# Memory attention of both layers in eight units of two heads, its sample sequences in 32-row blocks

## The reference, cut to what matters

```python
def memory_attention(qm, g_q_mem, mem_k, mem_v):
    B, L, _ = qm.shape
    q = rms_norm(qm.reshape(B, L, H_MEM, HD_MEM), g_q_mem)
    s = jnp.einsum('blhd,bmhd->bhlm', q, mem_k).astype(jnp.float32) * (HD_MEM ** -0.5)
    p = jax.nn.softmax(s, axis=-1)
    return jnp.einsum('bhlm,bmhd->blhd', p, mem_v).reshape(B, L, D_MEM)
```

## Time and profile before

| | us |
|---|---|
| median of 3 runs (2698.41 to 5250.33) | 2704.03 |
| the profiled execution, its whole time | 2707.99 |
| its span, first to last instruction | 2706.3 |
| TensorE busy in the span | 2585.6 (96%) |
| VectorE busy | 1182.1 (44%) |
| ScalarE busy | 810.8 (30%) |
| mean granted clock of TensorE, share of full speed | 0.965 |

### The profile page before, as it was taken

One profiled execution on the slowest core, in us unless ns is written; L12 is line 12 of the kernel. 1 busy time (PEld: TensorE's weight loads), 2 busy tenths in 40 slices (PEclk: granted clock), 3 DMA queues, 4 the chain that ended last, 5 costly groups with the idle time before them and its releaser, 6 DMA issues.

```text
span 2706.3 us, 44423 instructions
## 1 busy us (share of the span) xinstructions
PE 2585.6 (96%) x18995; PEld 2459.4 (91%) x18995; DVE 1182.1 (44%) x1455; ACT 810.8 (30%) x1019; POOL 101.5 (4%) x205
## 2 busy tenths in 40 slices
PE   6999999999988799999999999999998879999998
PEld 6999999999755599999999999999986559999998
DVE  7333335583354334433454343334543734443343
ACT  5222223443122323222233322222334633222222
POOL 1000000000112100000000100000011020000000
PEclk9999999999889789999999999999997989999999
DMA  5222322222212122223222322322232042223222
GB/s 175 82 85 73 91 80 75 62 67 80 60 56 74 61 63 78 74 82 93 72 68 94 115 78 81 87 80 70 89 121 75 26 146 78 78 69 102 78 60 84
DMA packets 334523, 220.74 MB, mean 82 GB/s; under 512 B 11849, under 2 KB 326497, under 8 KB 334420
## 3 DMA queue, kind: packets, MB, share of 16 engines
q1 hardware_dynamic: 325268, 185.83, 23.8%
q0 software_dynamic: 9152, 33.43, 3.8%
HBM read 206.78 MB, written 12.45 MB: 81 GB/s over the span
## 4 chain that ended last, share of the span: by engine, by line
PE 92%; DVE 5%; ACT 1%; issue 1%; DMA 1%; SPq 0%; POOLq 0%; POOL 0%; DVEq 0%; ACTq 0%
PE psum L519 73%; PE psum L545 6%; PE psum L2156 1%; PE psum L1443 1%; PE psum L1502 1%; PE psum L1494 1%; PE psum L1757 1%; PE psum L1483 1%; PE psum L1740 1%; PE psum L2379 1%; PE psum L1474 0%; PE psum L2202 0%; PE psum L1708 0%; PE psum L2185 0%; DMA x_nat<-in_x_sample 0%
## 5 line engine op out<-in xcount | busy, mean ns | idle before, releaser
L519 PE MATMUL psum<-act_hi,whi 128*128 128x288 f32 (+2 forms) x3504 | 756.1, 298 | 12.4 <-DVE act_lo L786 3.8
L519 PE MATMUL psum<-act_hi,wlo 128*128 128x288 f32 (+2 forms) x3504 | 753.8, 297 | 0.0
L519 PE MATMUL psum<-act_lo,whi 128*128 128x288 f32 (+2 forms) x3504 | 753.1, 297 | 0.0
L519 PEld LDWEIGHTS psum<-act_hi,whi 128*128 128x128 f32 (+2 forms) x3504 | 563.7, 188 | 15.3 <-issue 4.9
L519 PEld LDWEIGHTS psum<-act_lo,whi 128*128 128x128 f32 (+2 forms) x3504 | 564.0, 188 | 0.3
L519 PEld LDWEIGHTS psum<-act_hi,wlo 128*128 128x128 f32 (+2 forms) x3504 | 563.4, 187 | 0.4
L498 DVE TENSOR_TENSOR wlo<-raw,whi 128x2048 fp32r<-128x2048 f32 x190 | 435.4, 2292 | 238.7 <-ACT whi L491 238.5
L491 ACT ACTIVATE whi<-raw 128x2048 fp32r<-128x2048 f32 x190 | 362.0, 1905 | 272.6 <-PE psum L519 268.6
L519 PE MATMUL psum<-h_lo,whi 128*128 128x288 f32 x1408 | 301.9, 295 | 0.0
L519 PE MATMUL psum<-h_hi,wlo 128*128 128x288 f32 x1408 | 301.9, 295 | 0.0
L519 PE MATMUL psum<-h_hi,whi 128*128 128x288 f32 x1408 | 301.9, 295 | 0.0
(11 more groups left out here) (410 smaller groups left out, 2143.2 us busy)
## 6 DMA issues: line engine op xcount, KB each, us to landing
raw<-in_w_ffn_up SPq DMA_DIRECT2D x176, 512.0 KB, 5.0
raw<-in_w_ffn_down SPq DMA_DIRECT2D x64, 384.0 KB, 3.9
raw<-in_w_ffn_down SPq DMA_DIRECT2D x64, 320.0 KB, 3.4
raw<-in_w_out SPq DMA_DIRECT2D x16, 512.0 KB, 4.4
raw<-in_w_in_a SPq DMA_DIRECT2D x14, 512.0 KB, 4.7
raw<-in_w_in_a SPq DMA_DIRECT2D x16, 384.0 KB, 4.0
raw<-in_w_kv SPq DMA_DIRECT2D x12, 512.0 KB, 4.1
vpg<-in_cache_v POOLq DMA_DIRECT2D x16, 384.0 KB, 4.0
```

Of the source, the lines that this page charges most:

```text
L519: last = pe.matmul(psum[0:width, 4 * j + 2 * m + h, 0:HALF], w[:, k, cols], a[:, k, h * HALF:(h + 1) * HALF], start=(k == 0 and step == 0) ...
```

## The change

Both layers' prompt part goes by eight units u: 128 tokens (u // 2) and the two heads of one half of the partitions (heads u % 2 and 2 + u % 2). There are four slots for scores (PSUM banks 0 to 3), for the exponentials `ma_e` (in `spare_hi`) and for the turned ones `ma_pt` (in `spare_lo`), two for transposes (banks 4, 5) and outputs (banks 6, 7). The sample part turns keys 0 to 3 between units 4 and 7, keeps all 8 sequences' keys in SBUF (copied in place, half by ACT and half by DVE), makes scores and outputs of four sequences in four 32-partition blocks, the values streamed 256 columns wide, and turns the 128 x 256 result back in two transposes. The norm of the last mLSTM head moves on DVE behind the sample softmax of A. A's query norm uses the functions of B. A's memory loads move from POOL to SP, behind the state loads; the constants' making on POOL moves into the last head of the mLSTM; B's loads are all issued at once.

```diff
@@ PE @@
+            def scores(u):
+                t, rows = u // 2, slice(64 * (u % 2), 64 * (u % 2) + 64)
+                if u >= 4:
+                    pe.wait_ge(S.ma_exp, 8 * l + u - 3)
+                for x in range(2):
+                    last = pe.matmul(mem_scores(u)[:, x, :], B.qn[rows, x, t * P:(t + 1) * P], mk_t[l][rows, x, :],
                                      start=True, stop=True)
+            def turn(u):
+                pe.wait_ge(S.ma_p, 8 * l + u + 1)
+                if u >= 2:
+                    pe.wait_ge(S.ma_pt, 8 * l + u - 1)
+                for y in range(4):
+                    last = pe.transpose(psum[:, 4 + u % 2, y * P:(y + 1) * P], ma_e[:, u % 4, y // 2, (y % 2) * P:(y % 2 + 1) * P],
+                                        ident[:, :])
+            def outputs(u):
+                pe.wait_ge(S.ma_pt, 8 * l + u + 1)
+                if u >= 2:
+                    pe.wait_ge(S.ma_out_lo, 10 * l + u - 1)
+                for x in range(2):
+                    for m in range(2):
+                        h = 2 * x + u % 2
+                        last = pe.matmul(mem_mix(u)[:, x, :], mv[l][:, m, h * DM:(h + 1) * DM], ma_pt[:, u % 4, 2 * x + m, :],
+                                         start=(m == 0), stop=(m == 1))
+            def sample_scores(g):
...
+                for pair in range(2):
+                    for x in range(4):
+                        last = pe.matmul(psum[32 * x:32 * x + 32, 4 + g, 0:M], B.qz[:, pair, 4 * g + x, :],
+                                         keys_turned(B, 4 * g + x)[:, pair, :], start=(pair == 0), stop=(pair == 1),
+                                         skip_group_check=True)
+            def sample_outputs(g):
+                pe.wait_ge(S.ms_pt, 2 * l + g + 1)
+                pe.wait_ge(S.ma_out_lo, 10 * l + 7 + g)
+                for m in range(2):
+                    for x in range(4):
+                        last = pe.matmul(psum[32 * x:32 * x + 32, 6 + g, 0:M], ma_pt[:, g, m, 32 * x:32 * x + 32],
+                                         B.vs[:, 4 * g + x, m, :], start=(m == 0), stop=(m == 1), skip_group_check=True)
+            for u in range(4):
+                scores(u)
...
+            turn(0)
+            for u in range(8):
+                if u + 1 < 8:
+                    turn(u + 1)
+                if u + 4 < 8:
+                    scores(u + 4)
+                if u == 4:
+                    turn_keys(0)
+                    turn_keys(1)
+                if u == 6:
+                    turn_keys(2)
+                    turn_keys(3)
+                outputs(u)
+            sample_scores(0)
+            for b in range(4, 8):
+                turn_keys(b)
+            sample_scores(1)
+            for g in range(2):
+                turn_sample(g)
+                sample_outputs(g)
+            for g in range(2):
+                turn_back(g)
@@ ACT @@
+            exponents(0)
+            exponents(1)
+            for u in range(8):
+                if u + 2 < 8:
+                    exponents(u + 2)
+                copy_turned(u)
+                if u == 6:
+                    copy_keys(0)
+                if u:
+                    mixed_hi(u - 1)
+            copy_keys(1)
+            mixed_hi(7)
+            copy_keys(4)
+            copy_keys(5)
...
@@ DVE @@
             maxima(0)
+            hooks[0]()
+            maxima(1)
+            hooks[1]()
+            maxima(2)
+            for u in range(8):
+                weights_of(u)
+                if u + 3 < 8:
+                    maxima(u + 3)
+                if u == 3:
+                    place_memory_queries()
+                if u:
+                    mixed_lo(u - 1)
+            copy_keys(2)
+            copy_keys(3)
+            mixed_lo(7)
+            copy_keys(6)
+            copy_keys(7)
             for g in range(2):
+                sample_maxima(g)
+                sample_weights(g)
+            hooks[2]()
+            for g in range(2):
+                copy_outputs(g)
+            for g in range(2):
+                sample_lo(g)
@@ DVE, layer A @@
-            qnorm_dve(dve, 0, 2, 0, lambda k: qm_a[:, k, :], lambda k: MA.qn[:, k, :], lambda k: vec_t[:, 72:73])
-            head_norm_dve(dve, HA - 1, c)
-            mem_attention_dve(dve, 0, MA, c)
+            query_rinv_dve(dve, -1)
+            head_sums_dve(dve, HA - 1)
+            query_norm_dve(dve, -1, 0)
+            mem_attention_dve(dve, 0, MA, c, (lambda: None, lambda: None, lambda: head_norm_dve(dve, HA - 1, c)))
@@ SP, behind the state loads; POOL @@
+            for head, early in ((3, True), (4, False)):
+                sp.wait_ge(S.k_turned, head)
+                for what, bs in ((0, range(0, 6)), (1, range(1, 7))) if early else ((0, (6, 7)), (1, (0, 7))):
+                    for b in bs:
+                        memory_load(sp, 0, MA, what, b)
+                if i == (HA - 1) * NB:
+                    pool.wait_ge(S.k_turned, HA)
+                    query_picks_pool(pool, c)
```

More of the change, by code:

```diff
@@ L1672, in queries_b, with mem_scores @@
         def queries_b(k):
             return MB.qn[:, k, :] if k < 2 else qb_t[:, k - 2, :]
[L1681 to L1699 removed]
+        def mem_scores(u):
+            return psum[:, u % 4, :].rearrange("p (h m) -> p h m", h=2)
@@ L1789, in mem_attention_act, with exponents @@
-            mixed_hi(3)
+            def exponents(u):
+                at = 32 + 4 * (u % 4)
+                if u >= 4:
+                    act.wait_ge(S.ma_turned, 8 * l + u - 3)
+                act.wait_ge(S.ma_max, 8 * l + u + 1)
+                for r in range(2):
+                    ins = act.activation(ma_e[:, u % 4, r, :], mem_scores(u)[:, r, :], ACT.Exp, scale=scale,
+                                         bias=small[:, at + r:at + r + 1], accum_out=small[:, at + 2 + r:at + 3 + r])
+                ins.then_inc(S.ma_exp, 1)
@@ new lines, in sample_hi @@
+            def sample_hi(g):
+                act.wait_ge(S.ms_back, 2 * l + g + 1)
+                for x in range(2):
+                    for r in range(2):
+                        ins = act.activation(sample_mix(act_hi, x, r, g), mem_back(x, r, g), ACT.Copy)
+                ins.then_inc(S.ma_out_hi, 1)
+            exponents(0)
[8 more added lines that the diff above has]
+                    mixed_hi(u - 1)
@@ new lines, in maxima, with weights_of @@
+            def maxima(u):
+                dve.wait_ge(S.ma_scores, 8 * l + u + 1)
+                top = small[:, 32 + 4 * (u % 4):34 + 4 * (u % 4)]
+                step(dve.tensor_reduce(top, mem_scores(u), AX, ALU.max))
+                dve.tensor_scalar(top, top, -scale, None, ALU.mult).then_inc(S.ma_max, 1)
+            def weights_of(u):
+                sums = small[:, 34 + 4 * (u % 4):36 + 4 * (u % 4)]
+                dve.wait_ge(S.ma_exp, 8 * l + u + 1)
+                step(dve.reciprocal(sums, sums))
+                e = ma_e[:, u % 4, :, :]
+                dve.tensor_tensor(e, e, sums.unsqueeze(2).broadcast_to([P, 2, M]), ALU.mult).then_inc(S.ma_p, 1)
@@ new lines, in sample_weights, with copy_outputs @@
+            def sample_weights(g):
+                at = 49 + 2 * g
+                dve.wait_ge(S.ms_exp, 2 * l + g + 1)
+                step(dve.reciprocal(small[:, at:at + 1], small[:, at:at + 1]))
+                dve.tensor_scalar(ma_e[:, g, 0, :], ma_e[:, g, 0, :], small[:, at:at + 1], None, ALU.mult).then_inc(S.ms_p, 1)
+            def copy_outputs(g):
+                dve.wait_ge(S.ms_out, 2 * l + g + 1)
+                dve.tensor_copy(ms_nat[:, g, :], psum[:, 6 + g, 0:M]).then_inc(S.ms_nat, 1)
```

414 lines of the change are left out of this document (154 added, 260 removed).

## The result

| | before | changed |
|---|---|---|
| median, us | 2701.8 (10 runs) | 2721.8 (10 runs) |
| the profiled execution, us | 2708.0 | 2709.4 |
| its span | 2706.3 | 2707.7 |

The ratio is **1.0059**, 95% interval 1.0040 to 1.0078: some 16 us slower, far inside the 2%; the two medians are 20 us apart. One execution of before at 5250 us is left out of the ratio. 2710 was forecast, and the range of 2685 to 2735 holds the result. The profiled execution of the changed kernel was the fastest of its ten; the others lie at 2720 to 2723. So its trace understates the loss: the two profiled executions are only 1.4 us apart.

What follows compares the result with a forecast made beforehand. The prediction took TensorE's projections, left alone, as the bound (92% of the chain); only the attention stretches move: 37.6 - 19.8 - 12.1 = +5.7 us on 2708.0 gives 2713.7, the median 4.0 lower, 2710 us; range 2685 to 2735.

Steps and rivals of the forecast that it cites:

- the prompt part: Attention over the prompt in both layers: 39.6 us a layer against 21.6 and 20.0, together +37.6 us.
- the sample part: Attention of the samples in both layers: 18 us in A and 17 in B against 26.6 and 28.2, -19.8 us.
- the forecast case: The whole kernel at the forecast of 2710 us, between 2700 and 2720; chance 0.50.
- the ring: Prompt part: queue order makes each unit pay a full round through PE, ACT and DVE, 4.4 us (6.7 at lower clock).
- The rival that the halves overlap: Prompt part: a unit's scores cost 0.55 and outputs 0.6 us, 7 us less a layer, 2696 us; chance 0.15.
- The clock in it: Prompt part: mean clock 0.735, 47% of the time at full, between 32.9 us (full) and 48.3 (low) a layer.
- the lower clock throughout: Rival: PE at 1.2 GHz in both layers, prompt 96.6 us, sample 40.8, +24, 2734 us; chance 0.15.
- the higher clock's rival: PE at 2.4 GHz throughout, prompt 65.8 us, sample 31.7, -18 from the forecast, 2692 us; chance 0.15.
- The blocks do what they say: Sample products: four blocks run at once, 1.1 us a group; rival one after the other 4.1, 2734 us, chance 0.05.
- The front: Query norm to first probabilities: A 11.3 us instead of 23.1, B -0.3, together -12.1 us.
- The moves: A's loads to SP's queue, the constants earlier on POOL, B's early loads: costed at nothing.
- The rule weighed: First four units' scores: 2.0 us, halves side by side; under strict program order about 1 us later a layer, sum 2712.

Runs made afterwards that it cites:

- e4: The changed kernel with three unread products per unit put into PE's waits of the prompt part, order unchanged; 2695.1 us, ratio 0.9961.
- e12: The changed kernel with DVE taking the low part of unit u-2 instead of u-1; one run, 2684.3 us.
- e5: The changed kernel with the norm of the last mLSTM head put back on DVE ahead of A's memory attention; one run, 2717.7 us.
- e1: The changed kernel run again without any edit; 2717.3 us (6 runs), ratio 1.0053.
- e8: e3 with a step's four scores issued in head order 0, 2, 1, 3 instead of alternating halves; one run, 2667.6 us.
- e3: The changed kernel with the earlier prompt part: four steps of four heads, two buffers, old queue orders; 2667.2 us (5 runs), ratio 0.9866.
- e7: e3 with unread products put into PE's waits of the sample part, 48 in each layer; 2695.4 us, ratio 0.9972.
- e9: e6 with 12 unread products put into PE's waits of A's sample part alone; 2655.2 us, ratio 0.9822.
- e11: The kernel before the change run again without any edit; one run, 2698.7 us.
- e2: The changed kernel with DVE's low part of u-2 instead of u-1 and PE's scores ahead of the transposes; 2678.3 us, ratio 0.9902.
- e6: e3 with the queue orders of its four steps changed on PE, ACT and DVE to open the round; 2663.0 us (4 runs), ratio 0.9841.

## Why the prediction was right

The time was right, by its mechanism, and with two terms off in opposite directions for one reason, the clock. That they cancel for the most part is luck: the prompt part is 6.8 us above its term and the sample part 4.8 below. The range of 50 us was also wide for a forecast of +5.7, and the median of 2721.8 lies just above the 2700 to 2720 of the forecast case; what bears the mechanism out is the ring, and not the time.

**The ring: right, also in its price.** 6.7 us forecast at the lower clock, 6.87 above (5.05 on PE for 5.0, 1.82 for 1.7); 4.4 at the full one, 4.58 in e4. A unit's scores and outputs alone in their half took 1.13 and 1.09 us at the full clock (e12), 2.07 and 1.97 at the lower one, as taken from the earlier trace rows. The rival that the halves overlap is out. DVE idles for the high part, as it said, in six of A's eight units.

**The clock in it: the step that was mis-sized.** "The mean of the two clocks read, 0.735" was taken from stretches that the change replaces. Granted was 0.58. With that the prediction's own formula gives 1 / (0.16/32.9 + 0.84/48.3) = 44.9 us a layer; measured are 43.2 and 42.8. The term was +44.4 instead of +37.6. e4 shows the other end: 31.5 us at 1.00 for the 32.9 forecast. Neither rival of the clock describes both parts: the two prompt parts are 86.0 us, between the forecast's 79.2 and the 96.6 of the lower clock throughout, and the two sample parts 30.2, as the higher clock's rival had them (31.7).

**The sample part: -24.6 instead of -19.8.** The full-clock chain of 15.1 us is 14.5 in B; 17 was taken halfway to the lower clock's 20.4, and the clock was 1.00. The blocks do what they say; scores (and outputs) of four sequences took 1.07 us where 1.1 was forecast:

```profile
2071.47 1.07 PE L1712 MATMUL psum<-ma_ks,ma_qz 128*32 128x256 f32 x16 [0.99 <-issue]
```

**The front: -10.5 instead of -12.1.** From the last state 13.0 us instead of 11.3. The norm by quarters took 6.5 for 6.1, and 1.3 are a row that stood in the trace before and was not counted: ACT's loading of its exponential table. Before, it lay under DVE's head norm; now it comes behind the first maxima, on the path:

```profile
878.86 0.17 DVE L1865 TENSOR_SCALAR small<-small 128x2 f32<-128x2 f32 x1
...
879.13 1.28 ACT L1780 ACT_TABLE_LOAD   x1 [4.82 <-DVE small L1865]
...
880.43 0.47 ACT L1780 ACTIVATE spare_whi<-psum,small 128x256 f32<-128x256 f32 x1
```

By the Trainium skill, "ScalarE: Activation LUTs", What ACT_TABLE_LOAD costs, this is a real instruction of the engine's queue; the trace agrees, with 1.28 us. The norm that left the front earned 1.4 to 1.6 us there and cost 1.1 to 1.4 in the sample part (e5); 3.9 and 1.5 had been worked with.

**The moves: no cost seen, as said.** The rest of the kernel takes 2568 to 2574 us changed and 2570 to 2576 before, and from the end of A's attention to B's it is 1073.3 us before and 1072.8 changed. A's front begins 868.4 and 867.2 us after the start changed, 874.2 and 866.2 before.

**The sum.** 44.4 - 24.6 - 10.5 = +9.3 us for a forecast of +5.7, in the profiled pair; +9 to +15 over both executions of each, 12 between their means. The ratios say 16 us and, in e1, 14. In the profiled pair the rest of the kernel was 8 us shorter in the changed kernel, which hid the loss. What the slower nine executions have beyond the profiled one is open: no trace of one of them at 2721 us was taken, and e1's at 2717 us differs from it in the stick-breaking's first part most of all.

**The rule weighed.** The first four units' scores took 2.10 us in B at the full clock (2.0 forecast), and e8 shows directly that the halves go side by side. By the Trainium skill, "TensorE: Matmul & The Clock Gate", The mechanism, they would have taken 3.0, and the sum would have been 2712, nearer to the result but for a reason that these rows contradict. The ring kept PE busy 5.0 of each 6.87 us, with one wait of 1.86, and the clock still stayed at 1.2 GHz for 44 us on end in A, the first 11 of them in the front, and for 34 in B. By the Trainium skill, "TensorE: Matmul & The Clock Gate", HAM oscillation, bursts that are shorter than the waits between them drop the clock; here the bursts were longer than the waits, so the trace shows more than that rule covers. Nor does the 0.66 of before bear it out throughout: the prompt part began at the lower clock behind a wait of 7.87 us, but the clock fell once more at 911 us, among waits of 1 to 2 us.

## What to carry to other kernels

More slots don't pipeline a loop whose queues take the youngest result's tail before the next unit's head; look for the circle through all queues, and move its late member one round back. Opening one edge can leave a smaller circle behind it. A ring that lets PE wait a little in every round can cost twice, since the clock stays down with it: price it at both clocks, and take neither from a stretch that the change replaces. Small work of PE's in waits that nothing else can fill may pay, but only where the stage behind is bound by PE and has no waits of its own: 3.9 us behind A here for twelve products, and under 1 us behind B (91.0 us in e3, 90.2 in e7). A gain that shows hundreds of us behind an edit is to be looked for in a kernel without the edit before it is put down to it.

## What the runs showed of the hardware

- Unread products raise the granted clock: 0.58 to 1.00 in A's prompt part (e4), 0.54 to 0.88 and 1.00 behind A's sample part (e9, e7). A float32 product of 128 x 256 is two records and 0.48 us at the full clock.
- The busy share alone doesn't tell the clock: PE was busy 74% of the changed prompt part (31.9 of 43.2 us) at 0.58, 73% of that of before in e11 (13.55 of 18.6) at 0.85, and 98% in e2 at 0.70, where the first 16 of 26.3 us were at 0.50 with PE at work all through.
- The clock can fall inside a stage that begins at 1.00: in e7 8 us into the stick-breaking, behind waits of 0.47 and 1.44 us. That stage's first part took 82.0 us at 0.94 and 89.6 at 0.85 in two executions of the changed kernel, with the same sample part at 1.00 ahead of it, and 91.5 at 0.83 in e9. Some 580 us behind A's attention the trace of e6 has a low stretch, and those of e9 and e2 have none. What decides between these is open; the 7.6 us between the first two are more than half of what the change costs.
